# Paired score products, a multiply on GpSimd, interleaved memory units and rounded memory scores in a long transformer kernel

## The reference

```
# one recurrent head: a = cumulative sum of log f, k = 1 - f
o_inter = (q * exp(a))^T S
scores[t, s] = sum_k q[t,k] * exp(a[t,k] - a[s,k]) * k[s,k]   # s <= t
o = o_inter + scores @ v
S = exp(a_last) * S + sum_s (k * exp(a_last - a))[s] v[s]

# first block, end
h = h + (silu(conv(u)) * v) @ w_down ; h = rmsnorm(h)
# second block, layer i
mem_n = rmsnorm(mem) ; mkv = mem_n @ w_mem_kv[i] ; mk, mv = split(mkv)
q, k, v, qm = split(rmsnorm(x) @ w_in[i])
y_mem = softmax(qm mk^T / 8) mv        # 4 heads, 256 memory tokens
x = x + concat(y_tok, y_mem) @ w_out[i] ; x = x + ffn(rmsnorm(x))
```

## Time and profile before

| what | value |
|---|---|
| median of three runs | 2077.58 us (2073.34, 2077.58, 2078.3) |
| profiled execution | 2073.57 us, span 2071.8 us |
| PE busy | 2039.3 us, 98% of the span |
| DVE, ACT, POOL busy | 53%, 42%, 9% |
| granted TensorE clock | 0.999 of full speed in the mean; 0.94 in the last 42 us |

### The profile page before, as it was taken

The page is one execution under the profiler, slowest core; times in us unless marked ns, Lnnn a source line. Parts: engine busy times, 40 slices in busy tenths (PEclk is TensorE's granted clock), DMA queues, the critical chain, the costliest instruction groups (busy, mean ns, idle before and its releaser), DMA issues.

```text
span 2071.8 us, 32220 instructions
## 1 busy us (share of the span) xinstructions
PE 2039.3 (98%) x11899; PEld 1787.6 (86%) x11899; DVE 1092.4 (53%) x1805; ACT 868.1 (42%) x1350; POOL 185.1 (9%) x177
## 2 busy tenths in 40 slices
PE   8999999999999999999999999999999999999998
PEld 8999999999888988888988888888889888888887
DVE  4225777655663556566754433444556654433443
ACT  5434444543221544456733222334656643322333
POOL 0003000110110010001001100110014001100100
PEclk9999999999999999999999999999999999999999
DMA  4322111132333333332023332332322033333332
GB/s 135 105 82 81 42 42 42 52 92 87 96 102 110 88 91 98 92 115 72 1 70 93 92 107 85 94 110 80 103 84 62 23 99 94 99 94 91 93 102 79
DMA packets 321920, 174.99 MB, mean 84 GB/s; under 512 B 6560, under 2 KB 319136, under 8 KB 321840
## 3 DMA queue, kind: packets, MB, share of 16 engines
q1 hardware_dynamic: 321840, 173.92, 28.8%
HBM read 171.80 MB, written 2.10 MB: 84 GB/s over the span
## 4 chain that ended last, share of the span: by engine, by line
PE 68%; DVE 1%; issue 1%; ACT 0%; DMA 0%; POOL 0%; POOLq 0%; DVEq 0%; ACTq 0%
PE ps L1970 39%; PE ps L1976 19%; PE ps L2507 3%; PE ps L2474 2%; PE ps L2492 2%; PE ps L2452 1%; PE ps L2447 1%; PE ps L2543 0%; PE ps L2426 0%; DMA raw<-w_mem_kv 0%; DVE w_lo L1229 0%; PE ps L2088 0%; PE ps L2339 0%; ACT w_hi L740 0%; PE ps L2078 0%
## 5 line engine op out<-in xcount | busy, mean ns | idle before, releaser
L1970 PE MATMUL ps<-z_hi,w_hi 128*128 128x512 f32 (+2 forms) x2128 | 643.6, 343 | 2.0 <-DVE mv L1739 0.8
L1970 PE MATMUL ps<-z_lo,w_hi 128*128 128x512 f32 (+2 forms) x2128 | 634.5, 339 | 0.0
L1229 DVE TENSOR_TENSOR w_lo<-raw,w_hi 128x1024 fp32r<-128x1024 f32 (+2 forms) x298 | 384.6, 1291 | 441.6 <-ACT w_hi L740 440.0
L740 ACT ACTIVATE w_hi<-raw 128x1024 fp32r<-128x1024 f32 (+2 forms) x298 | 328.2, 1102 | 420.6 <-PE ps L1976 371.4
L1976 PE MATMUL ps<-z_hi,w_lo 128*128 128x512 f32 (+2 forms) x2128 | 443.8, 339 | 0.0
L1970 PEld LDWEIGHTS ps<-z_hi,w_hi 128*128 128x128 f32 x2128 | 366.4, 188 | 53.8 <-issue 5.3
L1970 PEld LDWEIGHTS ps<-z_lo,w_hi 128*128 128x128 f32 x2128 | 365.1, 188 | 44.8
L1976 PEld LDWEIGHTS ps<-z_hi,w_lo 128*128 128x128 f32 x2128 | 344.2, 188 | 45.2
L1970 PE MATMUL ps<-g_hi,w_hi 128*128 128x512 f32 (+1 forms) x539 | 209.4, 390 | 0.5 <-POOL g_lo L670 0.5
L1970 PE MATMUL ps<-g_lo,w_hi 128*128 128x512 f32 (+1 forms) x539 | 208.8, 389 | 0.0
L670 POOL TENSOR_TENSOR g_lo<-gv,g_hi 128x512 f32 x66 | 85.6, 1297 | 1073.0 <-ACT g_hi L1077 1073.0
(11 more groups left out here) (318 smaller groups left out, 2381.3 us busy)
## 6 DMA issues: line engine op xcount, KB each, us to landing
raw<-w_gate_up SPq DMA_DIRECT2D x88, 512.0 KB, 3.7
raw<-w_down SPq DMA_DIRECT2D x48, 704.0 KB, 4.3
raw<-w_in SPq DMA_DIRECT2D x44, 512.0 KB, 3.7
raw<-w_up SPq DMA_DIRECT2D x44, 512.0 KB, 3.7
raw<-w_out SPq DMA_DIRECT2D x24, 512.0 KB, 3.7
raw<-w_in_b SPq DMA_DIRECT2D x14, 512.0 KB, 3.6
raw<-w_in_a SPq DMA_DIRECT2D x12, 512.0 KB, 3.6
raw<-w_branch SPq DMA_DIRECT2D x8, 512.0 KB, 3.7
```

The source lines that it names most:

```text
L740: act.activation(w_hi[s][:, 0:width], raw[s][:, 0:width], ACT.Copy).then_inc(hi_done, 1)
L1229: dve.tensor_tensor(w_lo[s][:, 0:width], raw[s][:, 0:width], w_hi[s][:, 0:width].bitcast(F32), ALU.subtract).then_inc(lo_done, 1)
L1970: pe.matmul(out, w_hi[s][:, w0 + k * P:w0 + (k + 1) * P], rhs[:, lo:lo + width], start=a, stop=False)
```

## The change

It has four parts.

1. Recurrent heads. Chunks 3 and 4 are kept backwards in time on the key side, and a tile `X` is 536 columns wide: keys of all chunks in the first 272 (for the last two chunks only left halves are wanted, which go in the places of the right halves of the first two), queries in the last 264. A level then is two products of 128 keys by 128 queries. The values of chunks 3 and 4 are reversed once by a product with an exchange matrix. The multiply of `qe` with the queries moves from VectorE to GpSimd.
2. The eight memory units are interleaved with the eight down units of `down_b` (`MERGED`), with the norm's sums and spreads inside the later ones; the rescaling of the residual moves into the first query projection.
3. Memory queries and keys are split in a rounded part and a remainder like the others, memory scores are two rounded products, and VectorE multiplies by one and takes the maximum in one instruction.
4. In the value projections the last unit works on tokens 256 to 511 first, and the first unit of layer 1 leaves its fourth token block to the end; waits for the copies stand later.

```diff
@@ the layout of a level
-        X = [sb(at, f"X{i}", [P, T1]) for i in range(3)]
+        X = [sb(at, f"X{i}", [P, KEYS + HALF]) for i in range(3)]     # KEYS = META + SEQ // 2
+        def last_left(x, l):
+            h = 2 ** l
+            v = x[:, KEYS:T1].rearrange("p (c n s h) -> p c n s h", c=2, s=2, h=h)
+            return v[:, :, ::-1, 0, ::-1], v[:, :, ::-1, 0, h - 1:h].to_broadcast([P, 2, P // (2 * h), h])
...
             def sub(h, l):
-                dve.tensor_tensor(right, aright, ref, ALU.subtract)
-                dve.tensor_tensor(left, ref, bleft, ALU.add).then_inc(mx["sub"], 1)
+                dve.tensor_tensor(queries_of(x[:, :], l), aright, ref, ALU.subtract)
+                dve.tensor_tensor(first_left(x[:, :], l)[0], first_left(A[:, :], l)[1], first_left(B[:, :], l)[0], ALU.add)
+                dve.tensor_tensor(pair_right(x[:, :], l), last_left(A[:, :], l)[1], last_left(B[:, :], l)[0], ALU.add)\
+                   .then_inc(mx["sub"], 1)
...
@@ TensorE, scores of a level
-                for c in range(CHUNKS):
-                        out = bank[:, c * P // 2:(c + 1) * P // 2].rearrange("p (n h) -> p n h", h=2 ** l)
-                        queries = right_halves(rhs[:, lo:lo + P], l)
-                    x_ = pe.matmul(out, lhs[:, lo:lo + P], queries, start=True, stop=True)
+                    for c in range(2):
+                        x_ = pe.matmul(bank[:, c * P:(c + 1) * P].rearrange("p (g j) -> p g j", g=2),
+                                       x[:, META + c * P:META + (c + 1) * P],
+                                       x[:, KEYS + META // 2:].rearrange("p (g c j) -> p g c j", g=2, c=2)[:, :, c, :],
+                                       start=True, stop=True)
...
@@ ScalarE, exponentials of a level
-                act.activation(x[:, lo:], x[:, lo:], ACT.Exp).then_inc(mx["exp"], 1)
+                if l <= 3:
+                    meta, x = first_left(x[:, 0:KEYS], l)[0][:, 0:META // (2 * 2 ** l), :], x[:, META:]
+                    act.activation(meta, meta, ACT.Exp)
+                else:
+                    x = x[:, META // 2:].rearrange("p (b n) -> p b n", b=2)[:, :, META // 2:]
+                act.activation(x, x, ACT.Exp).then_inc(mx["exp"], 1)
...
@@ GpSimd, head
+                pool.wait_ge(mx["qe_exp"], 2 * h + 1)
+                pool.tensor_tensor(qe[:, :], qe[:, :], qf[:, 2 * h, META:], ALU.mult).then_inc(mx["qe"], 1)
@@ VectorE, head
-                dve.wait_ge(mx["qe_exp"], 2 * h + 1)
-                dve.tensor_tensor(qe[:, :], qe[:, :], qf[:, 2 * h, META:], ALU.mult).then_inc(mx["qe"], 1)
...
@@ TensorE, once, in the unit pinog 0
+                for c in range(2):
+                    x = pe.matmul(ps[3][:, c, :], exchange, V[:, 2 + c, :], start=True, stop=True)
...
@@ part 2
+        MERGED = [("down", 0), ("down", 1), ("mem", 0), ("down", 2), ("mem", 1), ("down", 3), ("mem", 2), ("down", 4),
+                  ("mem", 3), ("down", 5), ("mem", 4), ("down", 6), ("down", 7), ("mem", 5), ("mem", 6), ("mem", 7)]
+            def merged_squares():                       # ScalarE
+                for u, (kind, m) in enumerate(MERGED):
+                    act.wait_ge(used, n + u + 3)
+                    split_hi(n + u + 2, (n + u) % 2, WIDTHS[n + u + 2])
+                    if kind == "down":
...
@@ part 3, VectorE
-                dve.tensor_copy(ls(r, b)[:, 0:NMEM], banks(r + b)[:, 0:NMEM]).then_inc(s["ls"], 1)
-                dve.tensor_reduce(row_max[r][:, b:b + 1], ls(r, b)[:, 0:NMEM], AX.X, ALU.max)\
+                    dve.tensor_tensor_reduce(pairs_of(ls(r, b)[:, 0:NMEM]), pairs_of(banks(r + b)[:, 0:NMEM]),
+                                             ones.rearrange("p (o k) -> p o k", o=1).to_broadcast([P, 2, P]),
+                                             1.0, 3 * NEG, ALU.mult, ALU.max, row_max[r][:, b:b + 1])\
...
@@ part 4, TensorE
-                    if l and half:
-                        pe.wait_ge(*s.at("va", 1))
-                        pe.wait_ge(*s.at("vd", 1))
+                        first_unit, last_unit = l == 1 and not half and i == 0, final and i == count - 1
+                        groups = ((0, 1, 2), (3,)) if first_unit else ((2, 3), (0, 1)) if last_unit else ((0, 1, 2, 3),)
```

More of the change, by code:

```diff
@@ L23 @@
 HEADS = D // P
+KEYS = META + SEQ // 2
 VD = 64
@@ L1130, in rounded_heads @@
                     act.wait_ge(*s.at("scaled", m + 1))
-                    if m < queries:
-                        hi, tile = q_pair[0:HD, 2 * m:2 * m + 2, :], scaled_heads[m % 2][0:HD, :, :]
+                    if m < queries or m >= queries + keys:
+                        head = 2 * m if m < queries else 2 * (m - keys)
+                        hi, tile = q_pair[0:HD, head:head + 2, :], scaled_heads[m % 2][0:HD, :, :]
                     else:
@@ L1138, in layer @@
                     half = m % 2
-                    if 1 <= m <= queries + keys:
+                    if m:
                         rounded_heads(m - 1)
@@ L1150, in layer @@
                         heads = ps[half][j * HD:(j + 1) * HD, 0:1, :]
-                        if m < queries:
-                            x = act.activation(scaled_heads[half][0:HD, j:j + 1, :], heads, ACT.Copy, scale=HD ** -0.5)
-                        elif m < queries + keys:
+                        if queries <= m < queries + keys:
                             for rows in (slice(0, HD), slice(HD, P)):
@@ L1156, in layer @@
                         else:
-                            head = 2 * (m - queries - keys) + j
-                            x = act.activation(q_mem[0:HD, head:head + 1, :], heads, ACT.Copy, scale=HD ** -0.5)
+                            x = act.activation(scaled_heads[half][0:HD, j:j + 1, :], heads, ACT.Copy, scale=HD ** -0.5)
                     x.then_inc(ps_free[half], 1)
+                    if m == 3:
+                        act.wait_ge(mem_keys, 4)
+                        act.activation(mk_hi[:, :, :], mk_raw[:, MH * l:MH * l + MH, :], ACT.Copy).then_inc(s["mk_hi"], 1)
+                rounded_heads(queries + keys + 1)
                 n = UNITS[f"v{l}"]
@@ L1936, in layer @@
                         m = count * half + i
-                        if final:
-                            first = 8 * i // count
-                            front_blocks(first // 4, range(first % 4, first % 4 + 8 // count))
-                        if i == count - 1:
+                        first = 8 * i // count
+                        blocks = range(first % 4, first % 4 + 8 // count)
+                        if final and i == count - 1:
+                            front_blocks(1, blocks[:len(blocks) // 2])
+                            values_taken(half, count, width)
+                            front_blocks(1, blocks[len(blocks) // 2:])
+                        elif final:
+                            front_blocks(first // 4, blocks)
+                        elif i == count - 1:
                             values_taken(half, count, width)
```

541 lines of the change are left out of this document (317 added, 224 removed).

## The result

The changed kernel takes 2043.7 us (median of 4 runs, 2042.7 to 2044.7) where the kernel before takes 2076.9 on the same chip: ratio 0.9843, 95% interval 0.9826 to 0.986. That is 33.2 us less. I had forecast 2050 and a sum of 26.5, so the sign and the range of 2038 to 2062 hold, and 6.7 us of gain stand outside my sum.

What follows compares the result with a forecast made beforehand. TensorE, busy 98% of the span, was taken as the bound. The terms 11.7 - 1.8 + 4.4 + 8.1 + 4.1 gave 26.5 us off, about 2051 against the median of 2077.58; forecast 2050, bounds 2045 to 2056, with rivals 2038 to 2062.

Steps and rivals of the forecast that it cites:

- the first rival: Recurrent heads: TensorE stays the bound, VectorE is in time, part 1 gives 19.6 us or more: 2042; chance 0.16.
- The forecast mechanism: Recurrent heads: VectorE's chain from states to level 6 block leaves TensorE waiting 1.1 us before outputs; gain 1.37 a head.
- The mis-sized term: Recurrent heads: two products of 128 queries instead of four of 64 save 0.35 us a level.
- my upper bound of 0.40: Recurrent heads: saving per level, in us, if records cost the same whatever their width, half of 0.81.
- my own formula: Recurrent heads: VectorE 1.40 us earlier, less 0.23 for three added instructions, plus 0.20 of slack: 1.37 us a head.
- my 2.1: Last recurrent head: 2.1 of 2.45 us gained, with no successor's work in VectorE's way.
- the rival at 2060: Recurrent heads: GpSimd's multiply blocks VectorE for its whole length, 1.3 us a head, up to 10 us back; chance 0.05.
- the deciding point of a rival: Alternating memory and down units: TensorE waits for long units' splits unless these start at once; slower, 2085; chance 0.03.
- The 0 to 0.4 us for the norm's sums: Down units: the norm's sums may wait 0 to 0.4 us for VectorE's two additions for the last down tile.
- I had 1.7: Memory attention: waits for VectorE's last copy go as copy and maximum become one instruction, 1.7 us.
- not 0.2: Memory attention, first head: the fourth score block may wait 0.2 us as the last memory queries are rounded later.
- 0.65 saved in each layer: Before the first transposes: the waits go only in part, as ScalarE must first finish its split; 0.65 us each.

Runs made afterwards that it cites:

- run 1: Changed kernel with VectorE's level 6 score block taken right behind that of level 5, ahead of the next head's differences and key decays: 2035.8 us.
- run 5: Changed kernel with the multiply of the decayed queries back on VectorE in front of the diagonal, not on GpSimd: 2045.1 us.
- run 7: Changed kernel with the eight memory units in a row behind all eight down units instead of alternating: 2043.3 us.
- run 8: The kernel of run 7 with both engines splitting a down unit's next weights behind the work on its tile: 2047.3 us.
- run 9: The kernel of run 8 with TensorE waiting for the low parts of the weights before a memory key unit's first product: 2047.0 us.
- run 10: Changed kernel in its alternating order, with the splits behind the work on the tile: 2053.1 us.
- run 6: Changed kernel with each memory score block as one full-precision product instead of two rounded ones: 2050.2 us.
- Run 12: The kernel of run 1 with layer 0's last memory-query copy and scaling, and the first transposed block's copy, ahead of splits: 2033.8 us.
- run 2: The kernel before, with only VectorE's level 6 score block taken right behind that of level 5: 2075.9 us.
- run 4: Changed kernel with each level's two products taking only the forward chunk's 64 queries (results not right): 2044.1 us, a single run.

## Why the prediction was right, and where it was off

The number alone would speak for the first rival, at 2042: it said that no wait appears in the heads and part 1 gives 19.6 us. The trace rejects it, with seven waits of 1.26 us and 14.5 us in place of 19.6. The forecast mechanism is the one that is there. Of the 6.7 us outside the sum 2.9 are part 1, 2.3 the clock, and 1.5 small differences in the other stretches.

**Part 1** gave 14.5 us, not 11.7. The mechanism is the forecast one: a new wait before seven outputs, 1.26 us for my 1.1, because nothing idles in VectorE between the states and the block of level 6 (shown by run 1), and three added instructions of 0.07 us each. The mis-sized term is the level: I took 0.35 us saved, it is 0.44. I had spread the diagonal's 1.16 us, less the length of its last record, evenly over its records and got 0.13 us between starts; the first record is longer, and the others start 0.11 apart. The direct difference, the start of a level to the start of the gate product, was in the earlier trace rows as well, and half of its 0.81 was my upper bound of 0.40. Even that is too low: four records take 0.37 with the edge to the gate product. With 0.44, my own formula gives 4 x 0.44 - 0.23 + 0.20 = 1.73 us a head, and 1.8 is measured. The last head, with 2.6 us for my 2.1, follows too. The seventh head gave less, 0.96 (24.45 to 23.49): it alone has no pooled or normalising product on TensorE and was that much shorter before, while VectorE's chain now sets it like the others; TensorE waits 0.79 us more there, for the transposed keys' copy on ScalarE. The reversal cost 1.7, forecast 1.8.

**GpSimd's multiply** was booked at 0, and run 5 shows 0. The rule of the exclusive port pair (the Trainium skill, SBUF — State Buffer, Who interferes with whom), the rival at 2060, found no collision in the new place: VectorE has finished its split (264.43) when GpSimd starts the multiply (264.86). Elsewhere in the changed kernel's trace there is one: two VectorE instructions beside two GpSimd ones of 1.3 us each, where the memory queries of layer 0 are scaled:

```profile
936.12 1.83 DVE L1285 TENSOR_TENSOR w_lo<-raw,w_hi 128x1024 fp32r<-128x1024 f32 x1 [0.23 <-ACT w_hi L782]
937.87 1.84 DVE L1876 TENSOR_TENSOR scaled_heads<-scaled_heads,sig 64x1024 f32<-64x1024 f32 x1
...
940.84 1.22 DVE L1889 TENSOR_TENSOR q_pair<-scaled_heads,q_pair 64x1024 fp32r<-64x1024 f32 x1 [1.13 <-ACT q_pair L1188]
```
```profile
936.04 2.59 POOL L745 TENSOR_TENSOR bias<-att_con,con 128x384 f32<-128x384 f32 x2 [137.57 <-DVE q_pair L1889]
```

They take 1.83 and 1.84 us instead of 1.22, as their like take elsewhere: 0.6 more each, near the 0.5 of the earlier trace rows, and not the 1.3 of a full block. The measurement decides against the rule here.

**Part 2** gave 5.1 us for my 4.4. The sum was right, its reason half wrong. I said that the gaps go because a long unit stands beside a short one; run 7 shows that the order is worth nothing. Runs 8 and 9 show what kept the first gap, 2.15 us, away: the split ahead of the tile's work and the later wait for the low parts. For the other two, 2.0 us, the cause stays open; the own banks are the likely one. I had read the place of the split only as the deciding point of a rival, while it is worth 4 us in the row (run 8) and 9 in the alternating order (run 10). That the sum came out is in part luck, since the gaps went for another reason than mine. The 0 to 0.4 us for the norm's sums is 0.2: the products stop for it from 871.2 to 871.4. The moved rescaling cost nothing.

**Part 3** gave 8.5 for 8.1: 6.3 for the blocks (run 6), and 2.2 for the rest, where I had 1.7; the waits for VectorE's last copy are gone from the list.

**Part 4** gave 3.8 for 4.1, and is two errors that cancel. The fourth score block of the first head waits 1.25 us, not 0.2:

```profile
942.80 0.39 PE L2589 MATMUL ps<-k_hi,q_pair 128*128 128x256 f32 x1 [1.25 <-DVE row_max L1934]
...
952.16 0.63 PE L2652 MATMUL ps<-v_tok,pts 128*128 128x64 f32 x4 [0.86 <-ACT pts L1239]
```

The named mechanism is right, the last memory queries are rounded a step later. I hadn't followed the chain through: split, scaling, ScalarE's rounding, VectorE's rest. The first two have GpSimd beside them (rows above) and take 1.2 us longer than elsewhere, nearly the whole wait. Run 12 shows that the order removes the wait; whether keeping GpSimd away from these two would do it too was not tried. So layer 0 lost 0.5 us. In layer 1 the three waits (1.69 for the query copies, 1.28 for the values, 2.04 before the transposes) went but for 1.07 us, a gain of 4.3. The first transposes no longer wait; what is late next is the copy that the first values need, 0.86 and 1.07 us, as I had foreseen. I had 0.65 saved in each layer; it was 1.0.

**The median.** The terms give 26.5, the trace 30.9, the medians 33.2. The last 2.3 us are no work and no wait of the list: see the last section.

**A misreading without effect.** I wrote that TensorE's single gaps are 2 us at most. Two at the very start of the kernel before are 3.5 and 3.3 us, one for a load and one for VectorE; the change leaves them alone.

## What to carry to other kernels

Where products are short, count them, not their columns: pairing two of 64 columns brought a level from 0.81 to 0.37 us, although the operand had to be laid out in reverse for it. At 512 columns a record takes 0.43 us, so this ends where products are wide. When the bound engine gets shorter, walk the other engine's queue from its last input to the block that the bound engine needs next, and move everything that serves a later stage behind that block; here 1.38 us of such work cost 1.26 us a head, and moving it was worth 7.9 us. As long as TensorE's own work was the longer the same move was worth nothing (run 2). In a loop of weights that are split on the way, issue the split ahead of the work on the finished tile: it also frees the load's buffer.

## What the runs showed of the hardware

TensorE's clock falls after a short stop, in some executions. In the profiled execution of run 2, whose kernel is the one before but for one move on VectorE, and below it in the profiled one of the kernel before, the granted clock (the column behind POOL's) is:

```profile
860.00:880.00 20.00, 17.85 (x114) 16.57 (x114) 10.76 (x20) 10.42 (x17) 1.81 (x1) 0.91 0.29 87
1560.00:1580.00 20.00, 17.96 (x108) 17.77 (x107) 9.93 (x29) 11.02 (x25) 7.70 (x9) 0.91 0.33 81
```
```profile
860.00:880.00 20.00, 17.85 (x127) 16.62 (x126) 10.53 (x20) 10.73 (x18) 1.81 (x1) 1.00 0.30 91
```

The stretch of the kernel before holds the same gap of 2.15 us, at full clock. In run 2 the first stretch holds that gap, the second the one of 2.04 us:

```profile
1574.51 0.45 PE L2492 MATMUL ps<-con,ls 128*128 128x128 f32 x2 [2.04 <-issue]
...
1576.47 0.95 PE L2507 MATMUL ps<-v_tok,pts 128*128 128x64 f32 x4
```

Behind each, the products take nearly twice as long for some 3.5 us (the second row is 0.55 us in the earlier trace rows for a like one): TensorE runs at 1.2 GHz instead of 2.4. What such a fall costs in the end depends on what follows. Behind the second gap value products and heads take 1.6 us more than in the kernel before (112.61 against 111.02). Behind the first it is 0.6 (561.29 against 560.66), because a later wait shrinks from 1.22 us:

```profile
884.41 0.39 PE L1970 MATMUL ps<-mz_hi,w_hi 128*128 128x256 f32 x1 [0.38 <-DVE mv L1739]
```

Of 29 runs of the kernel before beside the experiments, 20 show a mean clock of 0.997 or lower and take 2075.6 to 2078.4 us; the five at 0.999 take 2073.3 to 2074.7. The profiled execution of the kernel before is of the second kind. The changed kernel has neither gap; its four runs show 0.999 at 2042.7 and 2042.8 us and 0.998 at 2044.6 and 2044.7. So the median of the kernel before lies 3.4 us above its profiled execution and that of the changed kernel 1.0 above, and the difference, some 2.3 us, is what a sum against one profiled execution doesn't see. That it is the clock in the executions without a profile is inferred from their mean clock.

Run 8 shows a fall as well (0.91 from 860 to 880 us, behind the wait of 1.91). Runs 9 and 10 have waits of 2.16 and 2.07 us, and their profiled executions show none. Runs 4 and 6 show one without such a wait, behind the norm's sixteen one-column records; run 6:

```profile
874.00:876.00 2.00, 2.00 (x13) 2.00 (x13) 1.12 (x8) 0.74 (x2) 0.00 (x0) 0.64 0.87 227
876.00:878.00 2.00, 2.00 (x12) 2.00 (x11) 1.05 (x3) 1.15 (x2) 0.00 (x0) 0.51 0.12 35
```

What decides in which executions it falls stays open.
